# A two-layer hybrid encoder step: layers written out, x loaded by column groups, operands made by VectorE alone, three weight chunks split ahead

## The chip, the cores and the metric

The kernel runs on one core of one Trainium2 chip. The metric is the device time in microseconds (us) of one execution. TensorE (PE) multiplies, VectorE (DVE) and ScalarE (ACT) work elementwise, GpSimd (POOL) does some sums and issues small DMAs, and SyncE (SP) issues the loads of the weights.

## The reference

The program is one inference step of an encoder trunk with two layers, for 256 prompt rows and 64 sample rows that share the weights (320 rows in all), with a width of 2048:

```python
def trunk_layer(x, pos, lw, past):
    h = rms_norm(x, norm1)
    proj = jnp.einsum('btd,de->bte', h, w_in)            # 2048 x 7264
    ...                                                  # sparse attention A, band attention B, state-space mixer C
    mix = jnp.concatenate([o_a.reshape(b, t, A_WIDTH), o_b.reshape(b, t, B_WIDTH), o_c], axis=-1)
    x = x + jnp.einsum('bte,ed->btd', mix, w_out)        # 2048 x 2048
    u = jax.nn.relu(jnp.einsum('btd,df->btf', rms_norm(x, norm2), w_up))      # 2048 x 8192
    x = x + jnp.einsum('btf,fd->btd', jnp.square(u), w_down)                  # 8192 x 2048
    return x, (ak, av, ik, b_k_rows, b_v_rows, h_last, conv_new)
```

After the two layers there is one final RMSNorm, and the new keys, values and states are stored as well. Everything is float32.

## The kernel before, in words

**Layout.** The residual stream is kept transposed, `xT` = 128 x 16 x 320: 16 feature tiles of 128 for 320 tokens. Every projection is a product of a weight block with an operand of 320 columns. To keep the precision of float32, weights and operands are split into a high and a low part, and each product is made of three matmuls: high x high, high x low and low x high (lines 682 to 684).

**Units and chunks.** A unit is 512 output columns of a weight matrix. It consists of 8 chunks of 2 feature tiles; one chunk is one DMA of 512 KB and 24 matmuls. A layer has 15 units for `w_in` (one of them small), the products with `w_out` in halves of 4 chunks, and 32 units for `w_up` and `w_down` (four quarters of 4 up and 4 down units). A unit accumulates in the four PSUM banks of `G`. DVE reads the low pair of banks as soon as the last chunk is done with it, and the high pair half a chunk later.

**Way of a chunk.** SP loads it into `raw` (a ring of 8). ACT copies it, rounded, into `whi` (`high_part`, line 1078, a ring of 4; it waits until PE has used the chunk four before). DVE subtracts `whi` from `raw`, which gives the low part in place (`split_chunk`, line 1344). PE waits for `split_done` before each chunk. DVE and ACT have one queue each, so the order in which the program lists their work is the order in which it runs.

**Order at a residual.** Around the end of a unit DVE first splits 2 chunks of the next unit (`next_unit`, or the range with `start + 2`), then reads the two pairs of banks into `xT` (`add_residual`, line 1504), then `new_operand` (line 1815): it tells ACT that the residual is new, waits until ACT has multiplied it by the norm weights (`weigh`, line 1043, four activations) and splits the result into `X_parts` (`split_operand`: a copy at line 1371 and a subtraction at line 1373). Only then come the further chunks. ACT squares the residual after `weigh` (line 1047), and POOL adds the squares to `SS4` (line 527). This happens 16 times: for the 4 column groups behind `w_out` and for the 4 behind the last quarter of `w_down`, in both layers; the operand is not made for the last of the 8.

**First unit of the MLP.** Here, between the splits for the next unit and the first read of `G`, DVE computes the reciprocal root of the norm (`make_rstd`, line 1378), for which POOL, PE (line 710) and ACT (line 1052) sum the squares.

**Start.** SP loads x in three DMAs of whole rows, then the weights; POOL's queue loads four tables of constants at the same time. PE turns x (line 733), ACT copies it to `xT`, weighs three of the four groups, and DVE splits them, while POOL squares and sums. Then PE begins its first unit; the fourth group is made inside the layer loop.

**Layers.** On all five engines a hardware loop (`Fori(0, DEPTH)`) runs over the two layers; semaphore targets are computed from the loop register. Inside it are short loops over the units of the MLP.

**End.** After the last residual ACT weighs and squares the fourth group, POOL adds, PE sums over the features, ACT and DVE make the reciprocal root, and PE turns `xT` back, from which ACT writes the scaled output that SP stores. DVE puts the weighed values into `xT` from `X_parts` (lines 1883 and 1886).

Of the kernel before, what the change touches and what calls it, by code (L numbers as in the profile page):

```python
# [19 lines left out]
F32 = mybir.dt.float32  # L20
F32R = mybir.dt.float32r
ALU = mybir.AluOpType
# [59 lines left out]
LAG = 2  # L82
Q_SMALL = [k for k, _, _ in PROJ].index("small")
# [120 lines left out]
def trunk(nc, x_prompt, x_sample, cache_a_k, cache_a_v, cache_a_kidx, cache_b_k, cache_b_v, state_ssm,  # L204
# [144 lines left out]
    weighed = Count(nc, "residual_weighed", 8, first=4)  # L349
    init_in = [sem(f"init_in{t}") for t in range(3)]  # L350
# [105 lines left out]
    def _(sp):  # L456
# [54 lines left out]
    def _(pool):  # L511
        pool.dma_start(seen[:], seen_in).then_inc(consts_in, 16)
        pool.dma_start(tri[:], tri_in).then_inc(consts_in, 16)
        pool.dma_start(ropeA[:], rope_in[0, 0:32]).then_inc(consts_in, 16)
        pool.dma_start(ropeI[:], rope_in[1]).then_inc(consts_in, 16)
# [4 lines left out]
        pool.memset(SS4[:], 0.0)  # L520
        pool.drain()
# [16 lines left out]
        pool.wait_ge(prm_ready.sem, 1)  # L538
        for j in range(3):
            x4 = xT[:, 4 * j:4 * j + 4, :]  # L540
            if j == 0:
                pool.tensor_tensor(SS4[:], x4, x4, ALU.mult).then_inc(ss_done.sem, 1)
                pool.drain()
                continue
            pool.tensor_tensor(sq, x4, x4, ALU.mult)
            pool.drain()
            pool.tensor_tensor(SS4[:], SS4[:], sq, ALU.add).then_inc(ss_done.sem, 1)
            pool.drain()
        pool.wait_ge(sq_done.sem, 4)
        pool.tensor_tensor(SS4[:], SS4[:], sq, ALU.add).then_inc(ss_done.sem, 1)  # L550


# [21 lines left out]
        with pool.Fori(0, DEPTH) as l:  # L574
# [83 lines left out]
    def _(pe):  # L658
# [66 lines left out]
        k = 0  # L725
        for t, (o, n) in enumerate(TILES):
            pe.wait_ge(init_in[t], 16)
            for i in range(4):
                if k >= 4:
                    pe.wait_ge(init_free[k % 4], k // 4)  # L730
# [7 lines left out]
        for b in range(4):  # L738
            pe.wait_ge(init_free[b], 4 if b == 0 else 3)
# [1216 lines left out]
```

## Time and profile before

| what | us |
|---|---|
| three timed runs | 3257.85, 3263.01, 3264.13 |
| their median | 3263.01 |
| span of the profiled execution | 3258.3 |
| PE busy in it | 3122.3 (96%) |
| DVE, ACT, POOL busy | 1711.3, 1151.3, 135.7 |

The span is the time from the first to the last instruction of the profiled execution; no other time of that execution is given. It lies 4.7 us below the median of the timed runs, and within their range. A busy PE is a PE with matmuls in flight. The granted clock of TensorE has two levels, 1.2 and 2.4 GHz, and is shown as a mean in parts of full speed for each stretch.

### The profile page before, as it was taken

What the parts mean: (1) busy time and instruction counts of PE and PEld (TensorE: products, weight loads), DVE (VectorE), ACT (ScalarE), POOL (GpSimd) and SP (SyncE); (2) the same over time, 40 slices, a digit from 0 to 9 for tenths busy, and PEclk for the clock granted to TensorE, in tenths of its full rate; (3) what the DMA queues carried; (4) which work ended last, traced back from release to release, by engine and by line L of the source; (5) the groups of instructions that cost most, each with busy time, mean ns of one, the idle gap of its engine ahead of it and who ended that gap; (6) DMA issues with size and microseconds to landing.
All of it is one profiled execution on the core that took longest, in us unless ns stands there. A gap on an engine that the chain in (4) does not pass through costs nothing.

```text
span 3258.3 us, 54928 instructions
## 1 busy us (share of the span) xinstructions
PE 3122.3 (96%) x20829; PEld 3064.7 (94%) x20829; DVE 1711.3 (53%) x2135; ACT 1151.3 (35%) x1376; POOL 135.7 (4%) x115
## 2 busy tenths in 40 slices
PE   6999999889999999999989999997999999999997
PEld 5899999689999999999989999986999999999997
DVE  5574467665434444444455745586644444444444
ACT  4333443233333333233323435422332333332333
POOL 4000000010000000000010000000100000000001
PEclk8999999799999999999999999997999999999999
DMA  6444443145455454454434544522454544544542
GB/s 201 125 146 126 143 143 113 57 123 146 150 150 148 148 149 149 150 150 149 130 109 131 153 143 126 155 89 64 128 151 150 149 148 148 149 150 149 150 141 79
DMA packets 233884, 444.64 MB, mean 136 GB/s; under 512 B 23073, under 2 KB 23521, under 8 KB 233425
## 3 DMA queue, kind: packets, MB, share of 16 engines
q1 hardware_dynamic: 228320, 426.37, 43.5%
q0 software_dynamic: 5424, 16.43, 1.6%
q8 instruction: 85, 1.39, 0.2%
q14 instruction: 55, 0.44, 0.0%
HBM read 430.94 MB, written 12.85 MB: 136 GB/s over the span
## 4 chain that ended last, share of the span: by engine, by line
PE 63%; issue 28%; DVE 5%; DVEq 1%; ACT 1%; POOLq 1%; DMA 0%; ACTq 0%; SPq 0%
PE G L682 19%; PE G L683 19%; PE G L684 19%; DVE raw_parts L1344 2%; PE M L719 1%; PE M L957 1%; PE M L851 1%; PE M L905 1%; ACT X L1043 1%; POOLq L528 0%; PE M L959 0%; DVEq L1372 0%; DVE xT L1504 0%; PE M L796 0%; PE M L777 0%
## 5 line engine op out<-in xcount | busy, mean ns | idle before, releaser
L1344 DVE TENSOR_TENSOR raw_parts<-raw,whi 128x1024 fp32r<-128x1024 f32 (+1 forms) x816 | 1013.3, 1258 | 884.5 <-ACT whi L1078 866.8
L1078 ACT ACTIVATE whi<-raw 128x1024 fp32r<-128x1024 f32 (+1 forms) x816 | 850.2, 1045 | 1469.5 <-PE G L684 1429.4
L682 PE MATMUL G<-X_parts,whi 128*128 128x320 f32 x3840 | 1200.2, 313 | 37.7 <-DVE raw_parts L1344 35.9
L684 PE MATMUL G<-X_parts,raw_parts 128*128 128x320 f32 x3840 | 1189.0, 310 | 0.0
L683 PE MATMUL G<-X_parts,whi 128*128 128x320 f32 x3840 | 1188.8, 310 | 0.0
L682 PE MATMUL G<-U_parts,whi 128*128 128x320 f32 x2560 | 805.1, 314 | 40.8 <-DVE raw_parts L1344 27.5
L683 PE MATMUL G<-U_parts,whi 128*128 128x320 f32 x2560 | 799.4, 312 | 0.0
L684 PE MATMUL G<-U_parts,raw_parts 128*128 128x320 f32 x2560 | 799.0, 312 | 0.0
L682 PEld LDWEIGHTS G<-X_parts,whi 128*128 128x128 f32 x3840 | 723.2, 188 | 44.6 <-issue 31.8
L683 PEld LDWEIGHTS G<-X_parts,whi 128*128 128x128 f32 x3840 | 723.3, 188 | 0.4
L684 PEld LDWEIGHTS G<-X_parts,raw_parts 128*128 128x128 f32 x3840 | 723.0, 188 | 0.0
L682 PEld LDWEIGHTS G<-U_parts,whi 128*128 128x128 f32 x2560 | 488.3, 191 | 47.9 <-issue 32.5
L683 PEld LDWEIGHTS G<-U_parts,whi 128*128 128x128 f32 x2560 | 488.5, 191 | 0.4
L684 PEld LDWEIGHTS G<-U_parts,raw_parts 128*128 128x128 f32 x2560 | 488.1, 191 | 0.0
L1504 DVE TENSOR_TENSOR xT<-xT,G 128x640 f32<-128x640 f32 (+1 forms) x96 | 78.5, 821 | 175.6 <-PE G L684 175.6
L527 POOL TENSOR_TENSOR SS<-SS,TB 128x1280 f32<-128x1280 f32 x16 | 62.7, 3918 | 1900.8 <-ACT TB L1047 1900.8
L1836 DVE SCALAR_TENSOR_TENSOR TB<-G,rstd 128x640 f32<-128x640 f32 x64 | 52.8, 825 | 119.2 <-PE G L684 119.2
L1291 ACT ACTIVATE U<-TB 128x640 f32 (+1 forms) x64 | 47.3, 739 | 87.5 <-DVEq L1838 87.5
L1043 ACT ACTIVATE X<-xT,prm 128x320 f32<-128x320 f32 x80 | 38.2, 551 | 65.4 <-DVEq L1817 65.3
L1373 DVE TENSOR_TENSOR U_parts<-U,U_parts (+1 forms) x64 | 52.9, 826 | 5.2
L1489 DVE SCALAR_TENSOR_TENSOR XC<-TB,prm,XC 128x323 f32<-128x323 f32 x96 | 46.8, 551 | 5.4 <-ACT XC L1249 5.2
L1117 ACT ACTIVATE XC<-M 128x384 f32<-128x384 f32 x32 | 15.7, 492 | 89.2 <-PE M L852 89.2
(270 smaller groups left out, 1354.5 us busy)
## 6 DMA issues: line engine op xcount, KB each, us to landing
raw<-in_w_up SPq DMA_DIRECT2D x256, 512.0 KB, 3.7
raw<-in_w_down SPq DMA_DIRECT2D x256, 512.0 KB, 3.6
raw<-in_w_in SPq DMA_DIRECT2D x224, 512.0 KB, 3.6
raw<-in_w_out SPq DMA_DIRECT2D x64, 512.0 KB, 3.6
U<-in_x_prompt SPq DMA_DIRECT2D x2, 1024.0 KB, 7.4
out_y_prompt<-U SPq DMA_DIRECT2D x8, 256.0 KB, 2.6
bias_ext<-XC POOLq DMA_DIRECT2D x2, 768.0 KB, 5.0
raw<-in_w_in SPq DMA_DIRECT2D x16, 80.0 KB, 2.0
```

Source lines behind the costliest of these rows:

```text
L527: pool.tensor_tensor(SS4[:], SS4[:], sq, ALU.add).then_inc(ss_done.sem, 1)
L682: pe.matmul(out, hi, xh, start=(i == 0 and k == 0), stop=False)
L683: pe.matmul(out, hi, xl, start=False, stop=False)
L684: mm = pe.matmul(out, lo, xh, start=False, stop=(c == part[1] - 1 and k == KC - 1))
L1043: ins = act.activation(X[:, 1, kt, :], xT[:, kt, :], ACT.Copy, scale=pcol(what, kt))
L1078: act.activation(whi[:, c % 4, :, cols], raw[:, c, :, cols], ACT.Copy).then_inc(high_done.sem, 1)
L1291: act.activation(U[:, 1, ds(4 * j + 2 * p_, 2), :], TB[:, 2 * p_ * TOK:(2 * p_ + 2) * TOK].rearrange("p (b t) -> p b t", b=2), ACT.Square)\
L1344: dve.tensor_tensor(wlo[:, c, :, cols], raw[:, c, :, cols], whi[:, c % 4, :, cols].bitcast(F32), ALU.subtract)\
L1373: return dve.tensor_tensor(parts[:, 1, tiles, :], full[:, 1, tiles, :], parts[:, 0, tiles, :].bitcast(F32), ALU.subtract)
L1489: dve.scalar_tensor_tensor(out=XC[:, kb, :], in0=xr[:, b, j:j + CONVOUT], scalar=pcol("cw", j * XB + kb), in1=XC[:, kb, :], op0=ALU.mult, ...
L1504: dve.tensor_tensor(x2, x2, pair(p_), ALU.add).then_inc((low_free if p_ == 0 else high_free).sem, 1)
L1836: ins = dve.scalar_tensor_tensor(out=t2, in0=pair(p_), scalar=0.0, in1=rb(), op0=ALU.max, op1=ALU.mult)
```

## The change

- The loops over the two layers are Python loops on all five engines: the code of a layer stands twice. The inner loops over MLP units stay.
- x is loaded in four column groups of 512 features (three DMAs each); the second to fourth group are issued among the first weight chunks. PE turns two groups ahead of the first unit, and the other two after its first and its second chunk. ACT copies a group, makes the high part of a weight chunk and squares the group; DVE makes the operand of a group, splits a chunk and adds the squares. POOL's squares and sums at the start are gone, and its four loads of constants wait for the first operand.
- `weigh` and `split_operand` for x are gone: `make_operand` on DVE makes the high part with four `tensor_scalar` and the low part with four `scalar_tensor_tensor`, of 320 columns each. ACT squares a residual at once.
- DVE splits `LEAD` = 3 chunks of the next unit, where it was 2, ahead of each read of `G`, and at the end of the first layer 3 chunks of the second layer's first unit, where it was none.
- At the end DVE multiplies `xT` by the norm weights in place, with 16 `tensor_scalar`.

```diff
+LEAD = 3
@@ SP
-        for t, (o, n) in enumerate(TILES):
-            src = x_prompt[0, o:o + n, :] if t < 2 else x_sample[0]
-            sp.dma_start(Uf[0:n, t * D_MODEL:(t + 1) * D_MODEL], src).then_inc(init_in[t], 16)
-        with sp.Fori(0, DEPTH) as l:
+        def load_x(i):
+            f = slice(i * UNIT, (i + 1) * UNIT)
+            for t, (o, n) in enumerate(TILES):
+                src = x_prompt[0, o:o + n, f] if t < 2 else x_sample[0, :, f]
+                sp.dma_start(Uf[0:n, t * D_MODEL + i * UNIT:t * D_MODEL + (i + 1) * UNIT], src).then_inc(init_in[i], 16)
+        load_x(0)
+        for l in range(DEPTH):
             for q, (kind, col, _) in enumerate(PROJ):
                 for c in range(CHUNKS):
+                    if l == 0 and q == 0 and 0 < c < 4:
+                        load_x(c)
...
@@ POOL
-        pool.wait_ge(prm_ready.sem, 1)
-        for j in range(3):
...
-        with pool.Fori(0, DEPTH) as l:
+        for l in range(DEPTH):
@@ PE
+        turn_x(0)
+        turn_x(1)
+        for l in range(DEPTH):
             def early(slot):
+                if l == 0 and slot < 2:
+                    turn_x(2 + slot)
                 if slot == 5:
...
                     sum_squares(l, 0, "ssq0")
@@ ACT
+        for l in range(DEPTH):
+            if l == 0:
+                for i in range(4):
+                    turned(i)
+                    if i < 3:
+                        high_part(l, 0, i)
+                    first_square(i)
+                act.wait_ge(ones_set, 4)
+            else:
+                high_parts(l, 0, 0, 3)
+                act.wait_ge(res_new.sem, res_new.at(l, 0))
+                act.wait_ge(ss_done.sem, ss_done.at(l, -1))
+                square(3)
...
                 act.wait_ge(res_new.sem, res_new.at(l, j + 1))
-                weigh(j, "mid")
                 act.wait_ge(ss_done.sem, ss_done.at(l, j))
                 square(j)
@@ DVE
         def next_unit(l, q):
-            chunks(l, q + 1, 0, 2)
+            chunks(l, q + 1, 0, LEAD)
+        def make_operand(j, what):
+            kts = range(4 * j, 4 * j + 4)
+            for kt in kts:
+                dve.tensor_scalar(X_parts[:, 0, kt, :], xT[:, kt, :], pcol(what, kt), None, ALU.mult)
+            dve.drain()
+            for kt in kts:
+                ins = dve.scalar_tensor_tensor(out=X_parts[:, 1, kt, :], in0=xT[:, kt, :], scalar=pcol(what, kt),
+                                               in1=X_parts[:, 0, kt, :].bitcast(F32), op0=ALU.mult, op1=ALU.subtract)
+            return ins
...
             for slot in range(SLOTS_AB + HALF):
                 q, c = slot // CHUNKS, slot % CHUNKS
-                split_chunk(l, q, c)
...
+                if l == 0 and slot < 4:
+                    first_operand(slot)
+                if l == 0 or slot >= LEAD:
+                    split_chunk(l, q, c)
+                if l == 0 and 0 < slot < 4:
+                    first_sums(slot)
...
                 dve.drain().then_inc(res_new.sem, 1)
-                if k < 7:
-                    dve.wait_ge(weighed.sem, weighed.at(l, k + 1))
-                    split_operand(X, X_parts, slice(4 * j, 4 * j + 4)).then_inc(ready.sem, 1)
+                if k < 7 or l < DEPTH - 1:
+                    make_operand(j, "mid" if k < 4 else "next").then_inc(ready.sem, 1)
             for j in range(N_OUT):
                 start = SLOTS_AB + HALF * j
-                for slot in range(max(start + 2, SLOTS_AB + HALF), start + HALF + 2):
+                for slot in range(max(start + LEAD, SLOTS_AB + HALF), start + HALF + LEAD):
                     split_chunk(l, slot // CHUNKS, slot % CHUNKS)
...
-            chunks(l, Q_MLP, 2, CHUNKS)
+            chunks(l, Q_MLP, LEAD, CHUNKS)
             next_unit(l, Q_MLP)
             make_rstd(l, 1)
             up_unit(l, Q_MLP, 0, 0)
...
             for j in range(N_UP):
                 q = UNITS - N_UP + j
-                chunks(l, q, 2, CHUNKS)
+                chunks(l, q, LEAD, CHUNKS)
                 if j < N_UP - 1:
                     next_unit(l, q)
+                elif l < DEPTH - 1:
+                    chunks(l + 1, 0, 0, LEAD)
                 add_residual(q + MORE, j, CHUNKS * (q + 1))
                 new_operand(l, j, 4 + j, x_in)
```

## Rows read from the trace of the kernel before

**Rows 1.** The page's first part: busy time, share of the span, instructions.

```profile
PE   3122.3 (96%) x20829; PEld 3064.7 (94%) x20829; DVE 1711.3 (53%) x2135; ACT 1151.3 (35%) x1376; POOL 135.7 (4%) x115
```

**Rows 2.** Waits of PE: who waited for whom, us in total, times, longest.

```profile
PE G L682 <- DVE raw_parts L1344: 63.4, 16, 23.1
```

**Rows 3.** Timeline of the start: start us, us, what [idle before <-releaser].

```profile
7.46 3.55 PE L733 MATMUL M<-ident,U 128*128 128x128 f32 x16 [7.46 <-DMA U<-in_x_prompt]
...
28.21 3.94 POOL L547 TENSOR_TENSOR SS<-SS,TB 128x1280 f32<-128x1280 f32 x1
...
38.47 0.63 PE L682 MATMUL G<-X_parts,whi 128*128 128x320 f32 x1 [23.06 <-DVE raw_parts L1344]
```

**Rows 4.** Stretches: PE, PEld, DVE, ACT, POOL busy, PEclk, DMA share, GB/s.

```profile
0.00:20.00 20.00, 6.89 (x49) 6.22 (x49) 2.04 (x2) 11.09 (x23) 8.21 (x15) 0.94 0.87 302
...
705.00:710.00 5.00, 3.02 (x12) 3.02 (x13) 5.00 (x4) 0.84 (x1) 0.85 (x1) 0.71 0.37 105
...
3145.00:3150.00 5.00, 2.65 (x11) 2.66 (x12) 5.00 (x4) 1.06 (x1) 1.10 (x1) 0.76 0.30 105
```

**Rows 5.** Timeline of DVE around two residuals behind `w_out`.

```profile
662.82 0.82 DVE L1504 TENSOR_TENSOR xT<-xT,G 128x640 f32<-128x640 f32 x1 [2.96 <-PE G L684]
...
679.38 0.82 DVE L1504 TENSOR_TENSOR xT<-xT,G 128x640 f32<-128x640 f32 x1 [2.22 <-PE G L684]
681.15 0.82 DVE L1504 TENSOR_TENSOR xT<-xT,G 128x640 f32<-128x640 f32 x1 [0.94 <-PE G L684]
...
686.38 3.98 DVE L1344 TENSOR_TENSOR raw_parts<-raw,whi 128x1024 fp32r<-128x1024 f32 x1
```

**Rows 6.** Timeline of ACT and of POOL around the second of them.

```profile
682.10 1.93 ACT L1043 ACTIVATE X<-xT,prm 128x320 f32<-128x320 f32 x4 [3.42 <-DVEq L1817]
683.94 1.26 ACT L1047 ACTIVATE TB<-xT 128x1280 f32<-128x1280 f32 x1
...
685.27 4.00 POOL L527 TENSOR_TENSOR SS<-SS,TB 128x1280 f32<-128x1280 f32 x1 [12.60 <-ACT TB L1047]
```

**Rows 7.** Groups of DVE by line and shape: busy us, mean ns, idle before.

```profile
L1765 DVE SCALAR_TENSOR_TENSOR MIX<-MIX,prm,TB 128x320 f32<-128x320 f32 x16 | 8.1, 549 | 0.6
...
L1611 DVE TENSOR_SCALAR U<-U,small_stats 128x256 f32<-128x256 f32 x8 | 2.3, 349 | 0.2
```

**Rows 8.** Timeline of PE: sums of squares in both layers, and the layer boundary.

```profile
61.04 2.32 PE L710 MATMUL M<-SS,ones 128*128 128x320 f32 x8
...
1639.28 0.63 PE L682 MATMUL G<-X_parts,whi 128*128 128x320 f32 x1 [8.35 <-DVE raw_parts L1344]
...
1661.88 2.32 PE L710 MATMUL M<-SS,ones 128*128 128x320 f32 x8
```

**Rows 9.** The chain that ended last, at the layer boundary: start us, us, what.

```profile
1632.20 4.04 issue
```

**Rows 10.** Timeline at the end of an MLP unit: DVE, ACT, weight loads of PE.

```profile
1024.32 1.23 DVE L1344 TENSOR_TENSOR raw_parts<-raw,whi 128x1024 fp32r<-128x1024 f32 x1 [2.29 <-ACT whi L1078]
1028.51 0.82 DVE L1836 SCALAR_TENSOR_TENSOR TB<-G,rstd 128x640 f32<-128x640 f32 x1 [2.96 <-PE G L684]
...
1026.74 1.06 ACT L1078 ACTIVATE whi<-raw 128x1024 fp32r<-128x1024 f32 x1 [2.46 <-PE G L684]
...
1029.92 0.19 PEld L682 LDWEIGHTS G<-X_parts,whi 128*128 128x128 f32 x1
```

**Rows 11.** Timeline at the end of the first MLP unit: DVE, then ACT.

```profile
744.58 2.15 DVE L1378 RECIPROCAL rstd<-STD 128x320 f32<-128x320 f32 x1
...
748.66 0.82 DVE L1836 SCALAR_TENSOR_TENSOR TB<-G,rstd 128x640 f32<-128x640 f32 x1 [0.94 <-PE G L684]
...
745.14 1.06 ACT L1078 ACTIVATE whi<-raw 128x1024 fp32r<-128x1024 f32 x1 [1.75 <-PE G L684]
```

**Rows 12.** Timeline of the end: ACT, then POOL.

```profile
3232.82 1.92 ACT L1043 ACTIVATE X<-xT,prm 128x320 f32<-128x320 f32 x4 [13.98 <-DVEq L1817]
...
3235.97 4.17 POOL L527 TENSOR_TENSOR SS<-SS,TB 128x1280 f32<-128x1280 f32 x1 [26.78 <-ACT TB L1047]
```

More of the change, by code:

```diff
@@ L348, in trunk @@
     usq_new = Count(nc, "usq_new", 8 * QUARTERS)
-    weighed = Count(nc, "residual_weighed", 8, first=4)
-    init_in = [sem(f"init_in{t}") for t in range(3)]
+    init_in = [sem(f"init_in{i}") for i in range(4)]
+    x_rows = sem("x_rows_turned")
     ident_in = sem("ident_in")
@@ L535, in clear_sums @@
             pool.drain()
-        pool.wait_ge(prm_ready.sem, 1)
-        for j in range(3):
[L540 to L550, printed above, removed]
+        pool.wait_ge(x_in.sem, 4)
         lead = P - 1
@@ L1037, in blocks @@
             return flat.rearrange("p (b t) -> p b t", b=4)[:, :, 0:n]
-        def weigh(j, what):
-            for b in range(BLKS):
-                kt = 4 * j + b
-                ins = act.activation(X[:, 1, kt, :], xT[:, kt, :], ACT.Copy, scale=pcol(what, kt))
-            ins.then_inc(weighed.sem, 1)
         def square(j):
@@ L1082, in high_parts @@
                 high_part(l, q + c // CHUNKS, c % CHUNKS)
-        with act.Fori(0, DEPTH) as l:
-            high_parts(l, 0, 0, 3)
-            act.wait_ge(res_new.sem, res_new.at(l, 0))
-            weigh(3, "next")
-            act.wait_ge(ss_done.sem, ss_done.at(l, -1))
-            square(3)
+        for l in range(DEPTH):
+            if l == 0:
+                for i in range(4):
[9 more added lines that the diff above has]
+                square(3)
             def mixers():
@@ L1385, in _, with first_operand, first_sums @@
             dve.sem_inc(banks.drained[b].sem, 1)
-        for j in range(3):
-            dve.wait_ge(weighed.sem, j + 1)
-            split_operand(X, X_parts, slice(4 * j, 4 * j + 4)).then_inc(x_in.sem, 1)
+        dve.sem_inc(ss_done.sem, 1)
         dve.sem_inc(layer_v.sem, 1)
+        def first_operand(i):
+            if i == 0:
+                dve.wait_ge(prm_ready.sem, 1)
+            dve.wait_ge(x_rows, i + 1)
+            make_operand(i, "next").then_inc(x_in.sem, 1)
+        def first_sums(i):
+            dve.wait_ge(sq_done.sem, i + 1)
+            dve.tensor_tensor(SS4[:], SS4[:], TB[:, 0:BLKS * TOK].rearrange("p (b t) -> p b t", b=BLKS), ALU.add)\
+                .then_inc(ss_done.sem, 1)
+            dve.drain()
         def rope_swapped(x, tab, rows, n):
@@ L1408, in rope_sum @@
             dve.tensor_tensor(x, x, TB[rows, 0:n * TOK].rearrange("p (b t) -> p b t", b=n), ALU.add)
-        with dve.Fori(0, DEPTH) as l:
+        for l in range(DEPTH):
             def place(kind, half):
@@ L1865, in _ @@
                     q = Q_MLP + 2 * N_UP * f + j
-                    chunks(l, q, 2, CHUNKS)
+                    chunks(l, q, LEAD, CHUNKS)
                     next_unit(l, q)
@@ L1880, in _ @@
             dve.wait_ge(sq_done.sem, sq_done.at(DEPTH, j - 3))
-            x4 = xT[:, 4 * j:4 * j + 4, :]
-            if j < 3:
-                ins = dve.tensor_tensor(x4, X_parts[:, 0, 4 * j:4 * j + 4, :].bitcast(F32),
-                                        X_parts[:, 1, 4 * j:4 * j + 4, :].bitcast(F32), ALU.add)
-            else:
-                ins = dve.tensor_copy(x4, X[:, 1, 4 * j:4 * j + 4, :])
+            for kt in range(4 * j, 4 * j + 4):
+                ins = dve.tensor_scalar(xT[:, kt, :], xT[:, kt, :], pcol("next", kt), None, ALU.mult)
             ins.then_inc(fin_new, 1)
```

82 lines of the change are left out of this document (35 added, 47 removed).

## The prediction, made blind

> **What bounds the kernel now.** I read the page's first part, then the waits of PE, then the timeline at each of them. PE is busy for 96% of the span, 136 us short of it [rows 1], so what an edit can gain lies in PE's pauses and in the time after them. Of the waits of PE one line is by far the largest: the first matmul of a chunk (line 682) waits for DVE's split (line 1344), 63.4 us in 16 pauses, the longest 23.1 [rows 2]. The longest is the start, where PE's first product comes at 38.47 [rows 3]; one of 8.35 is the layer boundary [rows 8]; the other 14 share 63.4 - 23.06 - 8.35 = 32.0, so 2.28 each. They stand at 7 residuals of each layer. All three kinds are touched by the change. Inside the units PE runs at 3.52 us a chunk: ACT's copy, which waits for one chunk of PE, shows 2.46 of idle and 1.06 of work [rows 10]. There nothing can be gained.
>
> **The residuals.** With t = 0 at the end of the high read, 681.15 + 0.82 = 681.97 [rows 5], the chain before is: ACT weighs from 682.10 for 1.93, squares from 683.94 to 685.20, POOL starts at 685.27 and ends at 689.27 [rows 6]; DVE copies and subtracts until 686.46, and its next split, begun at 686.38, takes 3.98 in place of 1.23 [rows 5, 10]. It ends at 690.36 with POOL's sum: the two engines exclude each other. POOL alone needs 689.27 - 686.46 = 2.8; before that it had waited for DVE. PE has two chunks of cover, 7.04 us, from 680.95 (0.20 ahead of the high read: the next unit's first matmul follows the last by 0.15, and the read follows its end). They end at 687.99, 2.4 too early.
>
> After the change the cover is 3 chunks, to 691.5, t = 9.5. DVE goes on at once. Its eight instructions cost 4 x 0.35 and a little more for 320 columns in place of 256, and 4 x 0.55 [rows 7], 3.6 end to end; as neighbours overlap by some 0.08, I take 3.3 (3.0 to 3.6). ACT squares without weighing, from t = 0.13 to 1.4, so POOL's sum now asks for its turn in the middle of the operand. I let it have it: 2.8 more. The operand is then ready at t = 6.2, later than before (4.5), and the fourth chunk's split at 7.4: 2.1 before PE asks for it. So the pause is gone, though the operand comes later; nobody needs that one before the next product with x.
>
> The Trainium skill speaks against this part: "SBUF — State Buffer", section "Who interferes with whom", says that a DVE instruction with two SBUF inputs and a GpSimd instruction hold one shared port pair in turn, the loser blocked for a whole instruction. The 3.98 agrees [rows 5]. By that rule all the gain would have to come from the third chunk, not from the shorter chain; the sum above has it so.
>
> What a pause costs in all: at 662.82 to 679.38 the low reads are 16.56 apart for four chunks, 14.08; 2.48 lost where the idle row says 2.26, so 0.25 more for each pause, 3.5 for 14 [rows 5]. And after four of the pauses (third behind w_out, first behind w_down, in each layer) the granted clock fell: 0.71 in the first such 5 us, 0.76 in the last, one of its levels being half speed [rows 4]. With the rest of the fall in the next 5 us that is about 1.5 each, 6.0. Gain of this part: 32.0 + 3.5 + 6.0 = **41.5**, if no pause remains.
>
> **The layer boundary.** PE restarts at 1639.28, and from there to the sum of squares it needs 22.60 for six chunks, 21.12 [rows 8]: 1.48 lost at half clock. With the idle 8.35 and 0.16 (a matmul's modelled end against its pace) 10.0 is lost. DVE's jump back to the head of the loop stands in the chain as 4.04 of issue [rows 9], and no chunk was split ahead. Written out there is no jump, and 3 chunks are ready; behind the last residual the same t = 7.4 against 9.5 holds, and the fourth operand is needed only at the seventh chunk. Gain **10.0**. The Trainium skill ("Runtime: NRT & Kernel Launch", section "Instruction fetch mechanics") says that a taken branch out of the fetched window stops an engine while straight code is prefetched; the 4.04 agrees. The straight body of a layer already runs without such a stop on PE.
>
> **The start.** Full-speed work began, in effect, at 61.04 - 21.12 = 39.92 [rows 8]. The trace shows POOL's sums between DVE's operands there (3.94 for one) [rows 3]; they go. New chain: a quarter of x is 640 KB. Before, 1 MB of x had landed at 7.46 [rows 3], and 0.38 MB less at 302 GB/s [rows 4] is 1.3 less; I take 6.5. PE turns 12 blocks at 3.55/16 = 0.22 (four of them smaller): 8.6. ACT's last copy and drain: 9.2. Operand 3.3, without POOL: 12.5; the first split: 13.7, first product. DVE is the bound from there: three times operand 3.3, split 1.15 and a sum like a subtraction of 1280, 1.5, make 18.0, and the split of the fifth chunk 1.2: 32.9; I add 0.9 where DVE must wait until PE has turned a group between chunks: 33.8. That is the start of the fifth chunk, so full-speed work begins in effect at 33.8 - 14.1 = 19.7. PE pauses several times on the way; at half clock a chunk takes as long again, and I add 1.3: 21.0. Gain **18.9**, between 14 (6.5 us of half-clock or late x) and 21 (no half clock). Loads of x and weights need 4.6 MB by then, 15 us at 302 GB/s, and hide. POOL's tables come after the first operand but are needed only behind the fifth chunk.
>
> **The end.** The weighing before the last square is gone: 1.92. POOL's sum took 4.17 [rows 12], of which 2.8 is its own time and the rest DVE's subtraction-sized instructions; now only instructions of 0.35 stand in its way. 1.9 + 1.1 = **3.0**.
>
> **What it adds.** In the first MLP unit DVE now splits a third chunk before `make_rstd`. ACT's copy of that chunk is 745.14 to 746.20, after PE's seventh chunk [rows 11], so it can't come sooner. Split to 747.4; reciprocal 2.15 to 749.5; low read 749.7 to 750.5. PE wants the banks at 748.66 - 0.20 - 0.15 = 748.3. Before, the reciprocal was done at 746.73 and the banks free in time. So PE pauses 2.2 in each layer: **-4.4** (0 if I misjudge the order, -7.6 with two falls of the clock).
> At every other unit end the third split also stands ahead of the low read: ACT's copy ends at 1027.80, the split (1.23) at 1029.05, the read (0.82) at 1029.80, against PE's next weight load at 1029.92 [rows 10]. Spare 0.1, less some hundredths for the semaphore. I take 0, bounds 0 and 0.2 at each of 70 unit ends: 0 to -14.
> The rest at nothing: register arithmetic that falls away between dependent steps of the mixers (a gain of at most some us), operands for the final norm that nobody reads, and loads, which stay under half of the DMA time.
>
> **Sum.** 18.9 + 41.5 + 10.0 + 3.0 - 4.4 = 69.0. The span 3258.3 becomes 3189.3; the span lies 4.7 under the median of the timed runs, so I forecast **3194.0**.
>
> **Rivals.** (a) The third split makes each low read late by some tenths: at 0.2, 14 us, **3208**. For: a spare of 0.1. Against: release to start takes hundredths in these rows. (b) The same mechanism on the other side: if the third split ran as long as the 3.98 one, each unit end would lose 2.7 and the kernel come out at 3194 + 70 x 2.7 = **3383**; it turns slower than before from 1.0 us a unit end on. Against: POOL is idle at nearly all of them. (c) The port: POOL's sum and DVE's eight instructions exclude each other more than once, or the operand takes 2.5 longer, and the pauses stay at half: **3215**. The page on SBUF named above allows it, as DVE has more instructions to lose with. (d) The start gives 8 to 10 only, because DVE's chain of four operands meets a half-speed PE: **3204**. (e) The code doesn't run as written, straight code fetched too slowly or the boundary still stopping: 10 to 60 lost, **3204 to 3254**. Against: a layer's body is straight already.
>
> **How the numbers follow.** Forecast 0.60 (own range 3184 to 3204), (a) 0.14, (b) 0.03, (c) 0.09, (d) 0.09, (e) 0.05. The range reaches down by the better bounds (start 2, first MLP unit 4, register work some us) to 3181 and up over (a), (d) and (c) to 3220. A measurement here can tell 0.2%, 6.5 us, from no change. Faster 0.94: all but (b) and the worst of (e); same 0.02; slower 0.04.
>
> **What would show it.** Right: no pause of PE for line 1344 behind the 14 residuals, and no fall of the clock there; first product at 13 to 16 us, the first sum of squares at 41 to 44; no pause at the boundary; two pauses of about 2 us behind the first MLP unit; POOL's sums overlapping the operand, one instruction of it stretched to some 3 us. Wrong: PE idle at every unit end before line 682, the wait put down to DVE's read of `G`; or the splits after a residual later than 9.5 behind the high read; or long gaps of issue on PE.

## The result, and the profile after

The changed kernel took 3178.94 us, the median of four runs (3173.47 to 3184.23), beside 3262.28 for the kernel before in the same series: a ratio of 0.9743, 95% interval 0.9731 to 0.9755, or some 83 us less. The forecast was 3194.0 with a range from 3181 to 3220. The direction and the mechanism came out; the size was 15 us short, and the measured median lies 2 us below the low end of the range.

The page's first part, of the execution that was profiled (span 3182.1, time 3184.23):

```profile
PE 3111.2 (98%) x20829; PEld 3055.1 (96%) x20829; DVE 1721.0 (54%) x2264; ACT 1115.8 (35%) x1296; POOL 99.9 (3%) x108
```

PE is now 71 us short of its span, where it was 136 short [rows 1]. ACT has 80 instructions fewer (the weighing) and DVE 129 more.

I cut both traces at the same marks on PE, each at the start of a matmul: a layer's first and last `M<-SS,ones` (the sums of squares; the last one belongs to the MLP's norm), the last `M<-MIX,ones` (the gate, which ends a mixer), and the final sum of squares. Times in us; the forecasts are the terms of the prediction's sum. (An expectation below says 8.6 us for the mixers, from marks rounded to 0.1; to 0.01 it is 8.4.)

| stretch | before | after | gain | forecast |
|---|---|---|---|---|
| start to the first sum of squares | 61.0 | 44.3 | 16.7 | 18.9 |
| the two mixers, from there to the last matmul of the gate | 580.2 + 580.2 | 577.4 + 574.6 | 8.4 | 0 |
| `w_out` and its residuals, into the first MLP unit, two layers | 99.9 + 99.9 | 87.1 + 87.0 | 25.8 | } |
| MLP of layer 0, the boundary, up to layer 1's sum of squares | 920.7 | 905.1 | 15.6 | } 50.1 |
| MLP of layer 1, up to the final sum | 898.2 | 889.7 | 8.5 | } |
| from there to the end | 18.1 | 17.0 | 1.1 | } |
| sum | 3258.3 | 3182.1 | 76.2 | 69.0 |

The last four stretches hold the residual pauses, the boundary, the end and the new pauses: 41.5 + 10.0 + 3.0 - 4.4 = 50.1 forecast, 51.0 measured. What the forecast missed in the trace is the row of the mixers.

**The residuals.** The waits of PE in the kernel after (who waited for whom: us in total, times, longest), which answer to [rows 2]:

```profile
PE G L675 <- DVE TB L1855: 3.8, 2, 1.9
...
PE G L675 <- DVE raw_parts L1341: 2.1, 1, 2.1
```

Line 1341 is the split (1344 before). Of its 16 pauses, 63.4 us, one of 2.1 is left, and that one stands in the start. All 14 behind residuals and the one at the boundary are gone. The first row is the new wait for the relu read in the first MLP unit, once a layer. DVE behind the second residual of `w_out`, which answers to [rows 5] (start us, us, engine, line, operation, what it reads and writes, idle before):

```profile
643.72 0.82 DVE L1523 TENSOR_TENSOR xT<-xT,G 128x640 f32<-128x640 f32 x1 [0.41 <-PE G L677]
644.73 1.27 DVE L1376 TENSOR_SCALAR X_parts<-xT,prm 128x320 fp32r<-128x320 f32 x4 [0.19 <-issue]
646.08 4.65 DVE L1379 SCALAR_TENSOR_TENSOR X_parts<-xT,prm,X_parts 128x320 fp32r<-128x320 f32 x4
650.66 3.48 DVE L1341 TENSOR_TENSOR raw_parts<-raw,whi 128x1024 fp32r<-128x1024 f32 x3
```

POOL in the same stretch, which answers to [rows 6]:

```profile
646.04 2.96 POOL L534 TENSOR_TENSOR SS<-SS,TB 128x1280 f32<-128x1280 f32 x1 [29.33 <-ACT TB L1038]
```

With t = 0 at the end of the high read (644.54), the operand is ready at 650.73, t = 6.2, and the first split is done at about 651.9, t = 7.3; the forecast said 6.2 and 7.4, and PE asks at 9.5. POOL's sum asks for its turn at 646.04 and takes 2.96 inside the four instructions of line 1379, which take 4.65 in place of the 1.94 that four of them take alone (the first operand of the start, below). So the operand comes later than before, as forecast, and nobody waits for it. The Trainium skill ("SBUF — State Buffer", section "Who interferes with whom") has DVE and GpSimd take the shared ports in turn; these two rows agree.

**The start.** PE, which answers to [rows 3]:

```profile
7.09 2.58 PE L728 MATMUL M<-ident,U 128*128 128x128 f32 x12 [3.92 <-DMA U<-in_x_sample]
13.37 2.59 PE L728 MATMUL M<-ident,U 128*128 128x128 f32 x12 [3.70 <-DMA U<-in_x_sample]
15.88 0.63 PE L675 MATMUL G<-X_parts,whi 128*128 128x320 f32 x1
```

DVE's first operand and split:

```profile
11.60 1.94 DVE L1379 SCALAR_TENSOR_TENSOR X_parts<-xT,prm,X_parts 128x320 fp32r<-128x320 f32 x4
13.46 1.22 DVE L1341 TENSOR_TENSOR raw_parts<-raw,whi 128x1024 fp32r<-128x1024 f32 x1
```

The first group landed at 7.09 (forecast 6.5), and its operand and split were done at 14.7. But the second group's turn stands ahead of the first unit on PE, and that group had landed only at 13.37, so the first product came at 15.88, not 13.7. The first sum of squares stands at 44.3, at the edge of the 41 to 44 forecast. Three more profiles with this start, below, have the second group at 12.5 to 12.6, the first product at 15.0 to 15.2 and the first sum at 42.5 to 44.1.

**The new pause.** Stretches of the kernel after (busy PE, PEld, DVE, ACT, POOL, then PE's granted clock, DMA share, GB/s):

```profile
720.00:725.00 5.00, 5.00 (x27) 5.00 (x27) 3.37 (x5) 1.90 (x2) 0.00 (x0) 0.72 0.05 7
2285.00:2290.00 5.00, 5.00 (x24) 5.00 (x25) 4.44 (x6) 2.29 (x3) 0.00 (x0) 0.66 0.20 74
```

Behind each of the two pauses of 1.92 the granted clock fell for a time to its lower level: the means over 5 us are 0.72 and 0.66. Idle and clock together cost more than the 4.4 forecast; the run with the earlier relu read, below, measures it.

### The profile page after: what moved, and what is told of

It reads as the page before. It is cut to its first block, busy times and chain, and to the rows that moved or that the text cites. A ratio compares the mean times of both kernels' runs of the same rounds, so it can differ in the third digit from the quotient of the medians.

```text
span 3182.1 us, 52698 instructions
## 1 busy us (share of the span) xinstructions
PE 3111.2 (98%) x20829; PEld 3055.1 (96%) x20829; DVE 1721.0 (54%) x2264; ACT 1115.8 (35%) x1296; POOL 99.9 (3%) x108
## 4 chain that ended last, share of the span: by engine, by line
PE 67%; issue 28%; DVE 3%; DVEq 1%; ACT 1%; POOLq 0%; DMA 0%; SPq 0%; ACTq 0%
PE G L675 20%; PE G L677 20%; PE G L676 20%; PE M L712 1%; PE M L955 1%; PE M L849 1%; PE M L903 1%; DVE raw_parts L1341 1%; PE M L957 0%; POOLq L535 0%; PE M L794 0%; PE M L775 0%; DVE X L1756 0%; PE M L703 0%; DMA U<-in_x_sample 0%
## 5 line engine op out<-in xcount | busy, mean ns | idle before, releaser
L1341 DVE TENSOR_TENSOR raw_parts<-raw,whi 128x1024 fp32r<-128x1024 f32 (+1 forms) x816 | 977.2, 1207 | 1085.5 <-ACT whi L1072 1071.7
L675 PEld LDWEIGHTS G<-U_parts,whi 128*128 128x128 f32 x2560 | 483.4, 189 | 15.0 <-issue 14.5
L676 PEld LDWEIGHTS G<-U_parts,whi 128*128 128x128 f32 x2560 | 483.5, 189 | 0.5
L534 POOL TENSOR_TENSOR SS<-SS,TB 128x1280 f32<-128x1280 f32 x16 | 47.6, 2976 | 1875.8 <-ACT TB L1038 1875.8
L1290 ACT ACTIVATE U<-TB 128x640 f32 (+1 forms) x64 | 47.4, 740 | 91.2 <-DVEq L1857 91.2
L1379 DVE SCALAR_TENSOR_TENSOR X_parts<-xT,prm,X_parts 128x320 fp32r<-128x320 f32 x76 | 77.4, 1077 | 1.5
```

The costliest lines, as they stand in the source:

```text
L675: pe.matmul(out, hi, xh, start=(i == 0 and k == 0), stop=False)
L676: pe.matmul(out, hi, xl, start=False, stop=False)
L1290: act.activation(U[:, 1, ds(4 * j + 2 * p_, 2), :], TB[:, 2 * p_ * TOK:(2 * p_ + 2) * TOK].rearrange("p (b t) -> p b t", b=2), ACT.Square)\
L1341: dve.tensor_tensor(wlo[:, c, :, cols], raw[:, c, :, cols], whi[:, c % 4, :, cols].bitcast(F32), ALU.subtract)\
L1379: ins = dve.scalar_tensor_tensor(out=X_parts[:, 1, kt, :], in0=xT[:, kt, :], scalar=pcol(what, kt), in1=X_parts[:, 0, kt, :].bitcast(F32), ...
```

## The experiments

Theory: the time went with the pauses that the third chunk covers (about 35 us with the new pause taken off), with the start (17), the end (3), and with writing the layers out, which gains at the boundary and, against the forecast, in the mixers. Rival: the mixers' 8.4 us are only another scatter of the clock, and what the layers gain is the boundary's alone. No run changes the start or the end alone: their gains are read off the traces.

**Layers alone.** The kernel before, with the loop over layers written out on all five engines:

```diff
-        with dve.Fori(0, DEPTH) as l:
+        for l in range(DEPTH):
```

(the same line for SP, POOL, PE and ACT)

> The kernel before with the layers written out on all five engines and nothing else. Theory A (the sum of the prediction): only the layer boundary gains. DVE splits the first chunk of the second layer directly behind the last residual, so PE restarts some 6 us earlier, with the fall of the clock there 6 to 7.5 us in all: about 3255 us. The stretch from the first sum of squares to the gate's sums stays as long as before in both layers (574 us). Theory B (the register arithmetic that falls away shortens the dependent steps of the mixers, the extra 8 us of the changed kernel's trace): that stretch gets 3 to 5 us shorter in each layer, about 3247 us.

Measured: 3241.33 us, ratio to before 0.9930 (0.9914 to 0.9947), some 21 us less; a second series of the same kernel is told below. That is more than both expectations. The stretch with the boundary went from 920.7 to 913.3, 7.4 us; the pauses behind the residuals all stayed. The other 13 us lie in stretches whose order of work did not change; in the trace the mixers have 9.2 of them, but unevenly (572.3 and 578.9).

**Three chunks alone.** The kernel before, with three chunks split ahead instead of two, the loop and ACT's weighing left as they were (and the same in the loops over `chunks`):

```diff
-            chunks(l, q + 1, 0, 2)
+            chunks(l, q + 1, 0, 3)
...
-                for slot in range(max(start + 2, SLOTS_AB + HALF), start + HALF + 2):
+                for slot in range(max(start + 3, SLOTS_AB + HALF), start + HALF + 3):
```

> The kernel before with three chunks split ahead in place of two, and nothing else: hardware loop, ACT's weighing and POOL's work at the start stay. Theory A: behind a residual the fourth chunk's split still ends 8.4 us after the high read, as the trace of before has it, against a cover of now 9.5: all 14 pauses go, 41.5 us, and the pauses in the first MLP unit come, 2.0 each and with two falls of the clock 7.4: 34 us gained, 3228 us; the start (first product at 38.5) and the layer boundary (8.35 idle) stay. Theory C (the operand on DVE alone is needed to make the third chunk tell): pauses of 1 us or more stay behind the residuals, 3240 us or more.

Measured: 3219.73 us, ratio 0.9873 (0.9857 to 0.9890), 42.8 less by the medians. The waits of PE:

```profile
PE G L682 <- DVE raw_parts L1344: 31.4, 2, 23.1
...
PE G L682 <- DVE TB L1836: 3.9, 2, 1.9
```

The two of the first row that are left are the start and the boundary: 14 pauses went through the third chunk alone, with ACT still weighing. The four stretches behind the gates, end left out, lost 11.5 + 11.6 + 6.4 + 7.2 = 36.7. This part gives half of the whole change, and it doesn't need the shorter operand. It is more than theory A's 34: the pauses of the first MLP unit came (the second row), but the granted clock didn't fall behind them. The stretch behind the first, which ended at 738.7:

```profile
740.00:745.00 5.00, 5.00 (x37) 5.00 (x36) 4.75 (x6) 2.55 (x3) 0.00 (x0) 1.00 0.20 42
```

**Two chunks in the changed kernel.** The same question from the other side:

```diff
-LEAD = 3
+LEAD = 2
```

> The changed kernel with two chunks split ahead in place of three. Theory A: behind a residual the third chunk's split ends 7.4 us after the high read (POOL's sum stands inside the operand), against a cover of 6.0: pauses of about 1.4 at 14 residuals and at the layer boundary, 15 x 1.65 = 25 with the 0.25 that each costs beside, some falls of the clock (6 to 15), less 7.4 for the two pauses in the first MLP unit, which go: 23 to 32 slower than the changed kernel, 3202 to 3211. Rival D (the shorter chain without ACT is what removed the pauses): no pauses, 3172.

Measured: 3192.66 us, ratio to before 0.9787 (0.9770 to 0.9803), 13.7 above the changed kernel. The waits of PE:

```profile
PE G L675 <- DVE raw_parts L1341: 20.9, 16, 2.1
```

The 13.7 are less than the 23 to 32 that theory A expected. The pauses are back, the boundary's among them, but at (20.9 - 2.1) / 15 = 1.25 each and not 2.28: the third chunk's split is done at t = 7.3 where it was done at 8.4 before. And the granted clock didn't fall behind them (0.98 in the `w_out` stretch, as in the changed kernel, where the kernel before shows 0.95), where theory A had 6 to 15 us for it. With the measured pauses and without that term its sum agrees: 15 x (1.25 + 0.25) - 7.4 = 15.1, and the same four stretches are 15.1 longer than in the changed kernel. So the third chunk is worth 36.7 us on the old operand and 15.1 on the new one, which has taken a good part already; both are net of what it costs in the first MLP unit.

**The kernel before, once more.**

> The kernel before as it is, for a second profile. If the difference between the two traces in the mixers (8.6 us) is the same program's spread, this profile has falls of the clock at other places and the stretch from the first sum of squares to the gate's sums differs from the first profile by some us; if not, it is 574.4 and 574.4 again, within 1 us.

Measured: 3257.57 us, span 3256.0, 1.6 apart. Its mixers took 579.4 and 577.4, where the first profile had 580.2 and 580.2.

**The changed kernel, once more, and its first MLP unit.**

> The changed kernel unaltered, profiled a second time and timed beside the kernel before, as the measure for the two kernels below that change its first MLP unit and its start. Theory A (the mixers became faster because instructions no longer compute loop-dependent values): the column-block stretch and the sweeps of layer 0 and 1 repeat the first profile to within 1 us wherever the granted clock is the same. Theory B (the mixers differ only by where the clock fell): at least one of the two layers gives back its 4 to 5 us in the column-block stretch. The median stays between 3173 and 3184 us.

Measured: 3181.05 us (3171.91 to 3184.11, five runs), ratio 0.9750 (0.9733 to 0.9767). The column-block stretch (the part of a mixer's state-space stage that goes through its twelve blocks, 523.1 to 619.3 us in the trace of before) took 93.9 and 90.7 us where the first profile had 95.2 and 90.8. Neither layer gave back 4 to 5 us, and layer 1 repeats at the same clock (0.98), as theory A has it. Layer 0 is 1.3 shorter at a higher clock, 0.95 against 0.93, which shows how much scatter there is.

> In the first MLP unit of each layer the next unit's first two chunks are split as before, but make_rstd and the unit's relu read now stand ahead of the third chunk's split instead of behind it. Theory A (the third split alone makes the relu read late, and the 1.92 us pause brings the clock down for some 1.8 us more): both pauses and both clock falls go, 7.3 us less than the changed kernel, ratio to it about 0.9977. Rival B: only the idle itself goes (3.9 us) because the clock falls somewhere behind it anyway. Rival C: the third split, now behind the read, is late for the third chunk of the next unit, and the pause only moves: 0.

```diff
-            next_unit(l, Q_MLP)
+            chunks(l, Q_MLP + 1, 0, 2)
             make_rstd(l, 1)
             up_unit(l, Q_MLP, 0, 0)
+            chunks(l, Q_MLP + 1, 2, LEAD)
```

Measured: 3174.97 us, beside 3181.05 in the same series; the intervals of the two ratios overlap (0.9729 to 0.9758, 0.9733 to 0.9767), so the medians alone don't settle it. The traces do. DVE at the end of the first MLP unit in the kernel after:

```profile
713.91 1.23 DVE L1341 TENSOR_TENSOR raw_parts<-raw,whi 128x1024 fp32r<-128x1024 f32 x1 [1.65 <-ACT whi L1072]
715.05 2.15 DVE L1385 RECIPROCAL rstd<-STD 128x320 f32<-128x320 f32 x1
717.28 1.79 DVE L1855 SCALAR_TENSOR_TENSOR TB<-G,rstd 128x640 f32<-128x640 f32 x2
```

The same in this kernel:

```profile
712.22 2.15 DVE L1385 RECIPROCAL rstd<-STD 128x320 f32<-128x320 f32 x1
714.56 0.82 DVE L1855 SCALAR_TENSOR_TENSOR TB<-G,rstd 128x640 f32<-128x640 f32 x1 [0.19 <-PE G L677]
...
719.90 2.35 DVE L1341 TENSOR_TENSOR raw_parts<-raw,whi 128x1024 fp32r<-128x1024 f32 x2
```

The read comes 2.7 earlier, PE has no wait for it, the stretches shown above stand at 1.00, and the two MLP stretches are 905.1 - 901.4 = 3.7 and 889.7 - 886.0 = 3.7 shorter. So each new pause costs 3.7 in this kernel, 1.92 of idle and the rest clock, 7.4 in all, as theory A had it (7.3): the forecast of the change took 4.4 and had 7.6 as its bound.

**The start: constants.** GpSimd's constant loads at once, as the kernel before had them:

```diff
-        pool.wait_ge(x_in.sem, 1)
         pool.dma_start(ropeI[:], rope_in[1]).then_inc(consts_in, 16)
```

> The changed kernel with GpSimd's four constant loads issued at once at the start, as the kernel before did, instead of behind the first operand. Theory A (the first product waits for the two first groups of x and the first weights, and the constants take a share of the same DMA engines): at the 302 GB/s of the opening the extra bytes move the first product from 15.9 to 17 to 18.5 us, the time by +1.5 to +2.5. Rival B (the opening is bounded by the latency of the transfers and the order of issue, not by bandwidth): the first product stays at 15.9, and the time within 0.5 us.

Measured: 3183.62 us (3177.28 to 3185.02), 2.6 above the changed kernel in the same series; the intervals of the two ratios overlap. The opening of PE:

```profile
8.89 2.59 PE L727 MATMUL M<-ident,U 128*128 128x128 f32 x12 [5.72 <-DMA U<-in_x_sample]
...
16.54 0.64 PE L674 MATMUL G<-X_parts,whi 128*128 128x320 f32 x1 [1.49 <-DVE raw_parts L1340]
```

The first group landed 1.8 later, the first product came at 16.54 (15.0 to 15.9 in the four profiles with the later constants), and the first sum of squares at 47.1 (42.5 to 44.3 there). That fits transfers that share bandwidth, theory A. By these traces the later constants are worth some 3 us: against the one of the four whose clock stood at the same 0.83 in 30 to 40 us, with its first sum at 44.1, it is 3.0. The first product itself moved less than to the 17 to 18.5 expected: the second group, which landed at 12.47, no longer held it, and DVE's split did.

**The start: second group first.** The kernel with the earlier relu read, and `load_x(1)` ahead of the first weight chunk:

```diff
         load_x(0)
+        load_x(1)
...
-                    if l == 0 and q == 0 and 0 < c < 4:
-                        load_x(c)
+                    if l == 0 and q == 0 and 0 < c < 3:
+                        load_x(c + 1)
```

> The kernel with the relu read ahead of the third split, and also the second group of x columns loaded ahead of the first weight chunk. Theory A (the turn of the second group, which landed at 13.4 us and stands ahead of the first unit on TensorE, holds the first product): the group lands about 2 us earlier, the first product comes at 14 to 15 instead of 15.9, and the time is 0.5 to 1 below the kernel without this edit. Rival B (the first weight chunk now lands later by the 0.9 to 2 us that the group takes, and its split becomes the last thing the product waits for): the first product at 15.9 to 17, the time 0 to +1.

Measured: 3173.79 us (3171.35 to 3174.62), ratio to before 0.9731 (0.9718 to 0.9744), the lowest median of all, but not told apart from the 3174.97 without this edit.

```profile
10.59 2.59 PE L729 MATMUL M<-ident,U 128*128 128x128 f32 x12 [0.78 <-DMA U<-in_x_sample]
14.87 0.63 PE L676 MATMUL G<-X_parts,whi 128*128 128x320 f32 x1 [1.70 <-DVE raw_parts L1342]
```

The kernel that it was edited from, with the earlier relu read alone:

```profile
12.51 2.59 PE L728 MATMUL M<-ident,U 128*128 128x128 f32 x12 [2.91 <-DMA U<-in_x_sample]
15.03 0.63 PE L675 MATMUL G<-X_parts,whi 128*128 128x320 f32 x1
```

Against that one the group came 1.9 earlier, but the first product only 0.2: it now waits for DVE's split, as rival B said, though not later than before. (It is 1.0 earlier than the 15.88 of the changed kernel's first profile, but that one is the latest of four with the same start.) The first sum of squares stood at 45.3, 1.2 later than the 44.1 of the kernel that it was edited from. The granted clock in 30 to 40 us doesn't explain it, 0.83 in both; the first chunk on PE does. In 14 to 20 us, of that kernel and then of this one:

```profile
14.00:20.00 6.00, 6.00 (x39) 5.55 (x37) 4.95 (x11) 3.63 (x6) 2.13 (x4) 1.00 1.06 292
14.00:20.00 6.00, 5.13 (x20) 5.13 (x21) 5.59 (x11) 3.29 (x5) 2.54 (x4) 1.00 1.06 344
```

PE had 39 matmuls there in one and 20 in the other, with the clock's column at 1.00 in both: here they start 0.27 us apart up to 19.6, there 0.15 apart from 16.4 on. The first chunk and the third group's turn took 7.1 us and not 5.5, and DVE's third operand began 1.2 later. Why the slow pace lasted longer is open; in these traces the edit gained nothing.

**Which engine's loop.** Four kernels of one series, all from the kernel before, with the layers written out on all engines, on VectorE alone, on TensorE alone, on ScalarE and VectorE (the diff of the first experiment, for those engines only).

> The kernel before with the layers written out on all five engines, profiled a second time, as the measure for the three kernels below that write out single engines. Theory A (writing out saves the jump at the boundary and, in every mixer, time in which the chain stands at an instruction whose loop-dependent values are being computed): boundary 913 instead of 921 us, the two mixers (sum of squares to gate) 3 to 4 us less each than the 577 to 580 of the profiles with a loop, 3241 within 4 us. Theory B (the mixers differ only by where the clock fell): the mixers back at 577 to 580, 3248.

> The kernel before with the layers written out on VectorE alone; the other four engines keep their loops. Theory A (VectorE's jump, 4.56 us between its last addition of layer 0 and its first split of layer 1, and its register arithmetic in the mixers make up nearly all of what writing out gains): boundary 913 to 915 us, mixers 2 to 4 us less each, 3242 to 3250. Theory B (TensorE's own jump and sequencing bound): boundary 921, mixers as with a loop, 3258 to 3263.

> The kernel before with the layers written out on TensorE alone. Theory A (VectorE's jump and register arithmetic are what stands on the chain): boundary 920 to 921 us, mixers within 1 us of those with a loop, 3258 to 3263. Theory B (TensorE's): boundary about 914, mixers 2 to 4 us less each, 3242 to 3250.

> The kernel before with the layers written out on ScalarE and VectorE. Theory A: as with VectorE alone and some 1 to 3 us less in the two mixers, where ScalarE's instructions stand on the chain too (its idle ended by issue fell from 26.5 to 16.2 us): 3239 to 3246, the same as with all five engines. Theory B (TensorE's jump and sequencing bound): 3258 to 3263.

| loop written out on | median us | ratio to before, 95% | stretch with the boundary | mixers |
|---|---|---|---|---|
| (none) | 3260.88 | | 920.7, 921.9 | 576.9 to 580.2 |
| all five | 3240.89 | 0.9949 (0.9932 to 0.9965) | 913.2 | 572.4, 572.2 |
| VectorE | 3246.97 | 0.9963 (0.9949 to 0.9977) | 913.6 | 572.6, 579.1 |
| TensorE | 3256.35 | 0.9987 (0.9978 to 0.9997) | 920.6 | 581.8, 576.2 |
| ScalarE and VectorE | 3246.19 | 0.9955 (0.9938 to 0.9971) | 913.6 | 576.9, 579.0 |

(The mixers of the first line are those of three profiles with the loop, three chunks alone among them.) At the boundary theory A came out in all four. In the mixers and the times it did so in part: with VectorE alone only one mixer is shorter, with TensorE alone one is 1.6 longer than any with a loop and the time is 2 us under its 3258 to 3263, and with ScalarE too the gain is not more than with VectorE alone. The boundary is settled: it is VectorE's jump. Its last addition of layer 0 and first split of layer 1, with VectorE alone written out:

```profile
1627.21 0.82 DVE L1504 TENSOR_TENSOR xT<-xT,G 128x640 f32<-128x640 f32 x1 [0.94 <-PE G L684]
1628.32 2.36 DVE L1344 TENSOR_TENSOR raw_parts<-raw,whi 128x1024 fp32r<-128x1024 f32 x2 [0.29 <-issue]
```

The same with TensorE alone written out:

```profile
1634.19 0.82 DVE L1504 TENSOR_TENSOR xT<-xT,G 128x640 f32<-128x640 f32 x1 [0.94 <-PE G L684]
1639.44 3.96 DVE L1344 TENSOR_TENSOR raw_parts<-raw,whi 128x1024 fp32r<-128x1024 f32 x2 [4.42 <-ACT whi L1078]
```

0.29 us of idle against 4.42, and 7 us at the boundary. The second row blames ACT, but ACT's copy is the same in both and ends 2.5 us ahead of the row above; the wait is the jump [rows 9]. The Trainium skill ("Runtime: NRT & Kernel Launch", section "Instruction fetch mechanics") says that a taken branch whose target isn't loaded stops the engine until it is fetched; these rows agree.

The mixers are not one thing. The chain of waits in layer 0's state-space stage (119.1 us long) of the kernel before, its shares by line:

```profile
by line: PE G L682 11.7%; PE G L684 11.2%; PE G L683 11.1%; PE M L957 8.8%; PE M L905 8.1%; PE M L959 6.5%; issue 4.4%; PE M L963 4.1%; DVE X L1737 3.3%; PE M L719 2.7%; ACT MIX L1212 2.2%; DVE X L1674 2.2%; PE M L899 2.1%; DVE X L1690 2.1%
```

The same (117.3 us long) in the second profile of the changed kernel:

```profile
by line: PE G L675 11.0%; PE G L677 10.5%; PE G L676 10.5%; PE M L955 9.6%; PE M L903 8.2%; PE M L957 7.2%; PE M L961 4.1%; DVE TB L1780 3.6%; DVE X L1756 3.4%; PE M L712 2.7%; issue 2.7%; ACT MIX L1212 2.2%; DVE X L1693 2.2%; DVE X L1709 2
```

Issue on the chain is 4.4% of 119.1, 5.2 us, before, and 2.7% of 117.3, 3.2 us, after: 2 us in which an engine stood at an instruction with nothing to wait for. That is where loop-dependent values were computed, and it was on the chain before. The runs with single engines bear this out. In the 118 us up to the gate, issue is 4.5% of the chain in both layers of the kernel before, 3.3 and 3.2 with VectorE alone written out, 2.8 and 2.8 with ScalarE too, 2.4 and 2.4 with all five, but 3.9 and 4.8 with TensorE alone. The changed kernel has 2.7 and 3.4. The rest is clock. The column-block stretch whole, with the columns of the stretches above, in layer 0 of the kernel before:

```profile
523.10:619.30 96.20, 90.19 (x537) 81.66 (x536) 72.49 (x157) 25.08 (x37) 1.99 (x3) 0.93 0.22 72
```

In layer 1 with TensorE alone written out:

```profile
2127.30:2218.50 91.20, 85.67 (x537) 77.60 (x536) 71.27 (x156) 25.06 (x37) 1.98 (x3) 0.98 0.24 76
```

In layers 0 and 1 of the changed kernel:

```profile
504.00:599.20 95.20, 90.00 (x537) 81.24 (x536) 71.41 (x156) 25.07 (x37) 2.00 (x3) 0.93 0.21 73
2075.00:2165.80 90.80, 85.36 (x537) 77.75 (x536) 70.97 (x156) 25.08 (x37) 1.97 (x3) 0.98 0.23 77
```

In layer 0 with all five written out (second profile):

```profile
521.00:611.50 90.50, 85.41 (x538) 77.81 (x536) 71.42 (x156) 25.08 (x37) 1.99 (x3) 0.98 0.24 77
```

At a granted clock of 0.93 (0.929 and 0.928) the stretch took 96.2 with VectorE's loop and 95.2 without; at 0.98 (0.981 in all three) it took 91.2 with it and 90.5 to 90.8 without. So the values cost 0.4 to 1.0 us in this stretch, and the clock 4.4 to 5.0. Outside it a mixer is 0.1 to 1.1 us shorter at equal clock. Over a whole mixer that gives 1 to 2 us, 2 to 4 of the 8.4 that the two gained; the rest of the 8.4 is that the clock stood less time at its lower level. The six mixers with all the loops took 576.9 to 580.2, 579 in the mean, the sixteen profiled with the layers written out on all engines 572.2 to 578.9, 575 in the mean; four of the sixteen reach into the range with the loops. That the clock falls less when VectorE's steps follow each other faster fits these rows, since the idle time by issue ahead of VectorE's sweeps (line 1690 before, 1709 after) fell from 6.3 to 4.9 us in 22 times, but no run isolates it: the same kernel shows 0.93 in one layer and 0.98 in the other. The last 6 us between VectorE alone and all five (by the medians; the intervals overlap) are open in the same way: in the `w_out` stretch, 101.4 at a clock of 0.93 against 98.4 at 0.97, with the same number of pauses.

## Why the prediction was right in direction and 15 us short

The miss has three parts: 3194.0 - 3178.94 = 15.1.

- **7.2 lie in the trace** (span 3189.3 forecast, 3182.1 measured: the mixers gained 8.4 more than forecast, the start 2.2 less, the rest 0.9 more). The step that failed is "the rest at nothing: register arithmetic that falls away between dependent steps of the mixers (a gain of at most some us)". The term measured 8.4, of which 2 to 4 are the arithmetic and the rest clock; why the clock fell less is open. It could have been bounded from the trace of before: the chain's share of issue in the state-space stage, 4.4% or 5.2 us a layer, was there to be read, and I read that chain only at the boundary. I had costed the written-out layers as one jump.
- **5.3 lie between the profiled run and the median.** The profiled execution of the changed kernel was the slowest of its four. Nine runs of it went from 3171.9 to 3184.2, at mean clocks of 0.989 to 0.985, so the runs of one kernel differ by 12 us, nearly as much as the 13 between the forecast and the low end of its range. Which of the four was profiled is luck.
- **2.6 lie in the offset.** I added 4.7 as "the span lies 4.7 under the median of the timed runs". In each execution whose time and span are both known, they are 1.5 to 2.7 apart (1.6 for the kernel before, 2.1 for the changed one). The other 3 us were scatter of the kernel before, which I carried over to the kernel after as if it were a cost outside the span.

Point by point:

- **The residuals** came out to a tenth of a us: operand at 6.2, split at 7.3, no pause. That the pauses end is the third chunk's doing, as forecast: it alone ends all 14. The run with two chunks adds what the sum had not asked: the new operand alone takes the pause from 2.28 to 1.25, as its split is done 1.1 earlier, no longer held by POOL's sum.
- **The boundary**: no pause is left. The jump alone gave 7.4 of the 10.0; the rest needs a split chunk in hand.
- **The start** gave 16.7 of 18.9. The mis-sized step is the arrival of x: the sum let the first product follow the first group, while the second group's turn stands ahead of it on PE, and that group landed at 13.37. Part of the 2.2 is scatter: in the second profile the group landed at 12.48 and the first sum stood at 42.5.
- **The end**: from DVE's last read into `xT` to the final sum on PE it takes 7.5 us before and 4.7 after, 2.8 of the 3.0 forecast. The 1.1 behind the final sum are not the edit's: the kernel with three chunks alone, with the old end, has the same 17.0 there.
- **The new pause** came, at 1.92 (forecast 2.2), and behind each of the two the clock fell; the forecast had that as a bound, 7.6. It could not be told ahead: of the 14 pauses of about this size before, four had a fall behind them, and of the two with three chunks alone none.
- **Rival (a)**, every low read late, fell: no wait for the relu read outside the first MLP unit. The spare of 0.1 us was enough. So did (b), which needed POOL at each unit end. **(c)** fell: one DVE instruction of the operand was held, once. **(d)** fell, and **(e)**: straight code stopped no engine.
- **The range** took the better bounds one by one, 2 + 4 + some us, and gave nothing for the scatter of runs. With that it would have reached to about 3170.

## What to carry to other kernels

Split far enough ahead that a late operand has cover, and then look what stands behind the extra split: here one order in one unit cost 7.4 us in the trace, and moving a single call returned them. Before costing a written-out loop as its jump, read the chain's share of issue inside the body, since values computed from the loop's variable stand on the chain wherever instructions depend on each other closely. Take the step from a trace to a time from one execution whose span and time are both known, and give the range the scatter of runs. Compare a run with the kernel that it was edited from, and in more than one profile: beside another profile of the start an edit seemed to gain 1.0 us, and beside its own base 0.2.

## What the runs showed of the hardware that I had not expected

- Pauses of PE of 1.25 us (15 of them, two chunks ahead) were followed by no fall of the granted clock; those of 1.92 to 2.3 by a fall in some places (4 of 14 before, both of the two in the changed kernel, none of the two with three chunks alone).
- One kernel has the same column-block stretch at 95.2 us and a mean clock of 0.93 in one layer and at 90.8 and 0.98 in the other. The 12 us between the runs of the changed kernel go with their mean clock: 0.985 in those of 3181 to 3184 us, 0.988 and 0.989 in those of 3172 and 3173.
- VectorE's jump to the head of a long loop stood as 4.2 to 4.6 us of idle in four profiles with its loop and was put down to ACT's copy; writing out VectorE alone took 7 us off the boundary, writing out TensorE alone none.
- In the opening PE's matmuls of 320 columns started 0.27 us apart, and later 0.15, while the granted clock's column says 1.00 for both.
